# A mixture-of-experts layer: expert rows summed per token in DRAM by scatters that add, and the last stage's odd tiles normed by ScalarE and GpSimd

## The reference

```python
top_logit, top_e = lax.top_k(logits, TOP_K)          # 4 experts per token
gates = jax.nn.softmax(top_logit, axis=-1)
...
xs = xf[tok]                                         # rows sorted by expert
hu = lax.ragged_dot(xs, w_gate_up, group_sizes) + b_gate_up[e_sorted]
gate = jnp.minimum(hu[:, :D_FF], SWIGLU_LIMIT)
up = jnp.clip(hu[:, D_FF:], -SWIGLU_LIMIT, SWIGLU_LIMIT)
act = (up + 1.0) * gate * jax.nn.sigmoid(SWIGLU_ALPHA * gate)
y = lax.ragged_dot(act, w_down, group_sizes) + b_down[e_sorted]
y = y * g_sorted[:, None].astype(y.dtype)
out = jnp.zeros_like(xf).at[tok].add(y)
...
h = layer_norm(ALPHA_RES * h + ffn, ln2_g[l], ln2_b[l])   # ALPHA_RES = 2 ** 0.25
```

## Time and profile before

| what | value |
|---|---|
| time, median of 3 runs | 4528.06 us (4527.1 to 4535.33) |
| profiled execution, span | 4529.3 us |
| PE busy | 4289.9 us (95%) |
| DVE busy | 3076.1 us (68%) |
| ACT busy | 1817.6 us (40%) |
| POOL busy | 1010.1 us (22%) |
| moved by DMA | 665.72 MB, mean 147 GB/s |

### The profile page before, as it was taken

The page is one execution under the profiler, slowest core; times in us unless marked ns, Lnnn a source line. Parts: engine busy times, 40 slices in busy tenths (PEclk is TensorE's granted clock), DMA queues, the critical chain, the costliest instruction groups (busy, mean ns, idle before and its releaser), DMA issues. The chain is left out here.

```text
span 4529.3 us, 70549 instructions
## 1 busy us (share of the span) xinstructions
PE 4289.9 (95%) x24356; PEld 3153.5 (70%) x24356; DVE 3076.1 (68%) x4861; ACT 1817.6 (40%) x2677; POOL 1010.1 (22%) x1152
## 2 busy tenths in 40 slices
PE   8999988999999998699999999999999999999987
PEld 4444434444444454599989889899999999999961
DVE  2587867878888873555556556666676777777768
ACT  1222223443434433233434444444445555555530
POOL 1111101221111122211112212222222222222235
PEclk9999989999999999799999999999999999999986
DMA  6443330120110010544555456474657667667668
GB/s 194 126 122 92 87 101 16 30 27 21 18 23 16 14 27 19 148 158 148 174 168 190 155 183 220 162 250 161 237 197 239 208 230 241 219 234 237 212 214 362
DMA packets 534140, 665.72 MB, mean 147 GB/s; under 512 B 64416, under 2 KB 402592, under 8 KB 533952
## 3 DMA queue, kind: packets, MB, share of 16 engines
q1 hardware_dynamic: 419664, 501.02, 34.7%
q10 hardware_dynamic: 87744, 77.15, 5.4%
q0 software_dynamic: 26576, 85.56, 5.0%
HBM read 543.61 MB, written 120.03 MB: 147 GB/s over the span
## 5 line engine op out<-in xcount | busy, mean ns | idle before, releaser
L2000 PE MATMUL gu<-x_hi,w_hi 128*128 128x240 f32 (+8 forms) x4096 | 1196.5, 292 | 4.1 <-issue 4.1
L2003 PE MATMUL gu<-x_lo,w_hi 128*128 128x240 f32 (+8 forms) x4096 | 1195.5, 292 | 0.5 <-issue 0.5
L2004 PE MATMUL gu<-x_hi,w_lo 128*128 128x240 f32 (+8 forms) x4096 | 1194.1, 292 | 0.0
L2106 DVE TENSOR_TENSOR w_lo<-w_raw,w_hi 128x2048 fp32r<-128x2048 f32 x386 | 874.6, 2287 | 414.1 <-ACT w_hi L2190 386.2
L2190 ACT ACTIVATE w_hi<-w_raw 128x2048 fp32r<-128x2048 f32 x386 | 726.8, 1908 | 207.4 <-PE gu L2004 132.0
L2000 PEld LDWEIGHTS gu<-x_hi,w_hi 128*128 128x128 f32 x4096 | 774.7, 189 | 4.5 <-issue 4.3
L2003 PEld LDWEIGHTS gu<-x_lo,w_hi 128*128 128x128 f32 x4096 | 773.3, 189 | 1.1 <-issue 0.9
L2004 PEld LDWEIGHTS gu<-x_hi,w_lo 128*128 128x128 f32 x4096 | 773.8, 189 | 0.0
L1972 POOL TENSOR_TENSOR a_lo<-up,a_hi 128x384 fp32r<-128x384 f32 x256 | 396.6, 1549 | 1177.8 <-ACT a_hi L2202 1177.8
L570 PE MATMUL proj_acc<-w_in_sb,hT 128*128 128x512 f32 (+1 forms) x1280 | 499.0, 537 | 0.7 <-ACT hT L586 0.7
L2000 PE MATMUL yp<-w_hi,a_hi 128*128 128x512 f32 x1088 | 445.6, 410 | 2.3
(11 more groups left out here) (316 smaller groups left out, 5878.6 us busy)
## 6 DMA issues: line engine op xcount, KB each, us to landing
w_raw<-w_gate_up SPq DMA_DIRECT2D x258, 1024.0 KB, 7.6
w_raw<-w_down SPq DMA_DIRECT2D x128, 1024.0 KB, 8.1
y_dram<-y_rows ACTq DMA_DIRECT2D x128, 256.0 KB, 2.6
y_dram<-zeros ACTq DMA_DIRECT2D x12, 2688.0 KB, 15.5
h_blk<-h_dram SPq DMA_DIRECT2D x32, 512.0 KB, 8.7
qi_dram<-qi_stage ACTq DMA_DIRECT2D x16, 640.0 KB, 3.2
x_in<-x SPq DMA_DIRECT2D x16, 512.0 KB, 6.1
w_in_sb<-w_in SPq DMA_DIRECT2D x4, 2048.0 KB, 14.2
```

The costliest lines, as they stand in the source:

```text
L2000: op = nc.tensor.matmul(out, s_hi_, m_hi, start=(n == 0), stop=False)
L2003: nc.tensor.matmul(out, s_hi_, m_lo, start=False, stop=False)
L2004: op = nc.tensor.matmul(out, s_lo_, m_hi, start=False, stop=(n == len(pairs) - 1))
L2106: nc.vector.tensor_tensor(w_lo[:, c % 2, cols], raw[:, c % 3, cols], w_hi[:, c % 2, cols].bitcast(F32), ALU.subtract).then_inc(s_lo, 1)
```

## The change

- In the attention stage `h1` is stored twice, once into `h1_dram` and once into `sums_dram`, where the experts' rows are to be added. 512 rows of zeros are put behind each of them (for list entries that stand for no token). An entry of `lists` is two numbers, token and gate, 8 bytes; the gates are divided by 2^0.25. The 12 DMAs that wrote zeros over most of `y_dram` in the projection stage are gone, as are `y_dram` and the position lists.
- In a visit, ACT's `store` scales a tile by the gates while copying (`gate_now`). POOL then issues an indirect DMA with `compute_op=ALU.add` that adds each row to its token's row in `sums_dram` (`scatter`; seven a visit, tile 2 by quarter rows). ACT's and SP's stores to `y_dram` are gone.
- The token numbers and gates for the scatters are made by `hold(v)` on POOL, which waits until all scatters of visit v - 1 have landed. `hold(v)` and `gather(v + 1)` stand between `a_lo` of step 2 and of step 3; `gather` stood at the start of the visit.
- SP loads the entries of the last 128 rows (`load_third(v + 1)`, five small DMAs), which waits for `hold(v)`, and stands ahead of chunk 5 of visit v.
- In the last stage a tile is one load from `sums_dram` into one of six buffers; PE adds only the bias rows; DVE does `sums` of all tiles and `finish` of the even ones in two instructions; odd tiles are normed by ACT (one instruction) and POOL (two).

The core of the diff:

```diff
@@ place_stage, weigh and project_stage (cut)
-                    nc.vector.tensor_copy(at_i[:], at_f).then_inc(s_at, 1)
+                    nc.vector.tensor_copy(at_i[:], at_f)
+                    nc.vector.tensor_copy(entry[:, :, 0], token[:, b:b + 1].broadcast_to([P, TOP_E]))
...
+                    nc.vector.tensor_scalar(entry[:, :, 1].bitcast(F32), e_gate, e_inv, 1.0 / ALPHA_RES,
+                                            ALU.mult, ALU.mult).then_inc(s_at, 1)
@@ experts_stage, SP
-                        if not first(v) and c in (3, 4):
-                            store_third(v - 1, 2 if c == 3 else 5)
+                        if c == 5:
+                            load_third(v + 1)
                         chunk(v, c, e)
+                def load_third(v):
+                    at = look_up(sp, v, 1, MOST)
                     rest, few = (look_up(sp, v, what, 1) for what in (2, 3))
+                    if not first(v):
+                        sp.wait_ge(s_hold, v)
                     for i in range(4):
+                        row = at + 2 * P + i * FEW - rest * ((i - i % 2) * FEW) - few * (i % 2 * FEW)
+                        sp.dma_start(third[i * FEW:(i + 1) * FEW], D_["lists"][bass.ds(row, FEW), :]
+                                     ).then_inc(s_third, 16)
+                    sp.dma_start(spot[:], A["spots"][bass.ds(rest + few, 1)].rearrange("o p j n -> (o p) j n")
+                                 ).then_inc(s_third, 16)
@@ experts_stage, POOL
+                def hold(v):
+                    if not first(v):
+                        pool.wait_ge(s_yst[0], 32 * v)
+                        pool.wait_ge(s_yst[1], 32 * v)
+                        pool.wait_ge(s_yst[2], 48 * v)
+                    pool.wait_ge(s_third, 80 * v + 80)
+                    nc.gpsimd.tensor_tensor(scaled[:], spot[:, :, 0], third[:, 0:1].broadcast_to([P, 3]), ALU.mult)
+                    for h in range(2):
+                        nc.gpsimd.tensor_scalar(at_main[:, :, h], who[:, 0:2, 0], 2.0, float(h), ALU.mult, ALU.add)
+                    nc.gpsimd.tensor_copy(gate_now[:, 0:2], who[:, 0:2, 1].bitcast(F32))
+                    nc.gpsimd.tensor_copy(gate_now[:, 2:3], third[:, 1:2].bitcast(F32))
+                    pool.drain()
+                    nc.gpsimd.tensor_tensor(at_third[:], scaled[:], spot[:, :, 1], ALU.add).then_inc(s_hold, 1)
+                    pool.drain()
+                def scatter(v, n):
+                    pool.wait_ge(s_y, 6 * v + n + 3)
+                    nc.gpsimd.tensor_tensor(idle[:, n:n + 1], zero[:, 0:1], zero[:, 0:1], ALU.add)
...
+                        nc.gpsimd.indirect_dma_start(rows, bass.IndirectOffsetOnAxis(ap=at, axis=0), part, None,
+                                                     compute_op=ALU.add).then_inc(s_yst[n % 3], 16)
                 def body(v):
-                    gather(v + 1)
+                    if not first(v):
+                        scatter(v - 1, 5)
                     for j in range(J):
+                        if j == 3:
+                            hold(v)
+                            gather(v + 1)
                         pool.wait_ge(s_ah, 8 * v + j + 1)
...
+                    for n in range(5):
+                        scatter(v, n)
@@ experts_stage, ACT
-                    nc.scalar.activation(y[:, slot], yp[:, n % 2], ACT.Copy).then_inc(s_y, 1)
...
+                    nc.scalar.activation(y[:, slot], yp[:, n % 2], ACT.Copy, scale=gate_now[:, slot:slot + 1]
+                                         ).then_inc(s_y, 1)
@@ combine_stage, SP and POOL
-                            rows[:, t % AHEAD, k], None, D_["y"],
...
+                def root(t):
...
+                    nc.gpsimd.tensor_tensor(shift, mean, rstd, ALU.mult)
+                    pool.drain()
+                    nc.gpsimd.tensor_scalar(shift, shift, -1.0, 1.0, ALU.mult, ALU.mult).then_inc(s_shift, 1)
+                def affine(t):
+                    row = total[:, t % AHEAD]
+                    pool.wait_ge(s_norm, t // 2 + 1)
+                    nc.gpsimd.tensor_tensor(row, row, gain[:], ALU.mult)
+                    pool.drain()
+                    nc.gpsimd.tensor_tensor(row, row, bias[:], ALU.add).then_inc(s_out[1], 1)
                 for t in range(TILES):
+                    root(t)
+                    if t >= 2 and t % 2 == 0:
+                        affine(t - 1)
+                affine(TILES - 1)
@@ combine_stage, DVE
                 def finish(t):
+                    if t % 2:
+                        return
+                    row, slot = total[:, t % AHEAD], t % SUMS
+                    nc.vector.scalar_tensor_tensor(row, row, small[:, slot, 12:13], gain[:], ALU.subtract, ALU.mult)
+                    dve.drain()
+                    dve.wait_ge(s_rstd, t // 2 + 1)
+                    nc.vector.scalar_tensor_tensor(row, row, small[:, slot, 15:16], bias[:], ALU.mult, ALU.add
+                                                   ).then_inc(s_out[0], 1)
```

More of the change, by code:

```diff
@@ L935, in attend_stage @@
         at_f = small[:, 58:62]
[L936 removed]
+        at_i, token, entry = S["at_i"], S["token"], S["entry"]
         e_gate = small[:, 62:66]
@@ L1979, in _ @@
                 n = over_visits(pool, body)
+                scatter(n - 1, 5)
                 pool.wait_ge(s_x, 48 * n + 48)
-                nc.gpsimd.tensor_tensor(who_now[:], who[:], zero[:], ALU.add)
+                pool.wait_ge(s_yst[0], 32 * n)
+                pool.wait_ge(s_yst[1], 32 * n)
+                pool.wait_ge(s_yst[2], 48 * n)
+                pool.wait_ge(s_third, 80 * n + 80)
+                nc.gpsimd.tensor_tensor(who_now[:], who[:, :, 0], zero[:], ALU.add)
             @block.tensor
@@ new lines, in root @@
+                def root(t):
+                    slot = t % SUMS
+                    mean, var_eps, rstd, shift = (small[:, slot, n:n + 1] for n in (12, 14, 15, 16))
+                    pool.wait_ge(s_var, t + 1)
+                    op = nc.gpsimd.tensor_tensor(rstd, var_eps, minus_half[:], ALU.pow)
+                    if t % 2 == 0:
+                        op.then_inc(s_rstd, 1)
+                        return
+                    pool.drain()
+                    nc.gpsimd.tensor_tensor(shift, mean, rstd, ALU.mult)
+                    pool.drain()
+                    nc.gpsimd.tensor_scalar(shift, shift, -1.0, 1.0, ALU.mult, ALU.mult).then_inc(s_shift, 1)
@@ L2428, in _ @@
                                          ).then_inc(s_bts, 1)
+                for t in range(1, TILES, 2):
+                    row, slot = total[:, t % AHEAD], t % SUMS
+                    act.wait_ge(s_shift, t // 2 + 1)
+                    nc.scalar.activation(row, row, ACT.Identity, bias=small[:, slot, 16:17],
+                                         scale=small[:, slot, 15:16]).then_inc(s_norm, 1)
 def build(nc, A, upto=9):
```

287 lines of the change are left out of this document (100 added, 187 removed).

## The result

The changed kernel takes 4540.4 us (median of six runs, 4531.6 to 4545.7), the kernel before 4528.8 us in the same comparison; the ratio is 1.0023, with a 95% interval of 1.0013 to 1.0033. The forecast was 4515 us and faster. The time lies inside the range, and the sign is wrong.

A forecast was written before the change was run, and what follows sets the result against it. PE alone was taken to hold the experts stage, the DMA engines the last stage. Terms +1 +4 +13 +0 +2 -33 = -13 us on the span of 4529.3 gave 4516.3, stated as 4515; range 4486 to 4562.

The forecast's parts named there:

- One visit, POOL: Experts stage, moved fetch on POOL: +1.1 us in each of 12 narrow visits, sum +13 us, bounds 0 and +85.
- the term `hold`: POOL, ahead of the fetch in a visit: six small instructions and two drains, about 1.2 us.
- the 12.0 us: POOL between steps 2 and 3: `hold`, look-up, row fetches, `a_lo` and `a_rest` together, releasing step 3's `a_lo` at 4141.1.
- d: Lateness of DVE's `up` of step 5 in a narrow visit: 1.7 us, said as 1.9 with one wait of `who_now`.
- 0.80 us of slack: DVE's idle time ahead of `gate` of step 7 in a narrow visit, taken off the lateness: chain end 1.1 us late.
- Visits of other widths: Wider visits of the experts stage: longer steps give 1.6 us of slack, so no cost; nothing changes in visits of 77.8 us.
- The rows' arrival: Narrow visit: third fetch lands at 4147.5 against the transposes at 4149.40; nothing, at most 0.6 us inside the 1.1.
- the scatters: Experts stage: landing taken as 6 us, no cost per visit; the last one waited for at the end, +2, bounds 0 and +6.
- Start: Start of the experts stage: five DMAs 3.0 us and look-ups 1.5, less two selects 0.7; +4, bounds 0 to +8.
- The last stage: Expert-row fetches go and a pair of tiles takes 11.0 us: -33 us, bounds -50 and -28.
- the mutual block: Last stage: POOL's affine and DVE's finish block each other, a pair taking 11.0 us instead of 8.6.
- the fetch rival: Step 3's `a_lo` late as `hold` meets `w_lo`: 3.1 us a narrow visit, 41 instead of 13, 4543; chance 0.27.

The follow-up runs named there:

- the writing scatter: Changed kernel with the scatters writing instead of adding (`compute_op=ALU.add` left out): 4536.3 us, ratio 1.0004 to the kernel before.
- the kernel before with `hold`'s like: Kernel before with the next visit's fetch moved to step 3, behind small operations and drains as in `hold` on unread tiles: 4578.0 us, ratio 1.0102.

## Why the prediction was wrong

**The step that failed is "One visit, POOL", and in it the term `hold`.** It was costed as six small instructions and two drains, 1.2 us; in every narrow visit it took 3.45. Of the 2.25 us between, 0.7 are there without any meeting (1.92 us in the wider visits, 0.98 of it idle ahead of the instruction behind the drain), and 1.5 come from meeting DVE, above all the `w_lo`. The other terms of the 12.0 us were right within 0.5: look-up 1.60 against 1.5, `who` to the first row 3.67 against 4.15, three fetches 3.74 against 3.9. So d was 3.35 and not 1.9, and each narrow visit lost 3.0 us and not 1.1. The mechanism was the one forecast (step 3's `a_rest` late, DVE's `up` of step 5 behind it, 0.80 us of slack, PE's wait put down to `a_rest`). That this place alone makes the loss is shown from both sides: put into the kernel before it costs 5 us a narrow visit, and spread in the changed kernel 0.1 to 0.35 are left.

The prediction had the case among its rivals, with 3.1 us for a narrow visit and 1.4 for the next width, 41 us in all; measured were 3.0, 0.4 and 38.8 (35.8 up to the last visit, and its own 3.0). It weighed it low by one sentence: "by my count `hold` is through 0.1 us before" the `w_lo` that blocks. By its own numbers that is not so: `a_rest` of step 2 ended at 4129.09, 1.2 us more is 4130.3, and the `w_lo` began at 4130.11. And it put next to nothing for the drain, behind which the last instruction stands 0.98 us idle. A margin of 0.1 us in a sum of operations that the trace doesn't have is no margin: with the 1.92 us of the wider visits `hold` would end at 4131.0, in the middle of that `w_lo`, and the rival was the forecast. As for the rule of the Trainium skill's page "SBUF — State Buffer", section "Who interferes with whom", that the later of the two engines waits for the whole instruction of the other: the trace agrees: `at_third`, 0.20 us without a `w_lo` beside it, took 1.22 and ended with `w_lo` (4154.32 and 4154.26).

**Visits of other widths**: those of 77.83 us unchanged, as forecast; the width of 256 lost 0.4.

**The rows' arrival, the scatters**: neither is what PE waits for; the scatter lands in 7.4 to 7.6 us (median; the longest found in any of these traces is 10.2) against the 6 estimated, under the 12.4 from which it would cost. The end of the stage took +4 for it and not +2; the writing scatter shows that 3 of it are the addition. The Trainium skill's page "Collectives: The Full Stack", section "Stop ④ — SDMA + CCE: where bytes move and the add happens", has one pass with two reads; in these runs that pass lands in 7.6 us against 5.7 without the addition.

**Start**: +4 was forecast, +1.2 is in the profile once attention's own spread is taken out. The five small DMAs took 2.72 us (SP, 1851.96 to 1854.68), as forecast (3.0); where the 1.5 us of look-ups went the rows don't show:

```profile
1851.96 2.17 SPq L1901 DMA_DIRECT2D third<-lists_dram  x4
1854.33 0.35 SPq L1903 DMA_DIRECT2D spot<-spots  x1
1854.88 1.03 SPq L1884 DMA_DIRECT2D w_raw<-w_gate_up  x2
```

**The last stage** is the part that was right in size: -37 against -33. Pairs came every 10.6 to 10.9 us (11.0 forecast), the first in 8.7, by the mutual block; the chain that ended last (start us, us) runs over POOL with its two affine rows and the drain behind the root (L2328), which the count had not had:

```profile
4448.90 2.32 POOL total L2336
4451.35 3.36 POOL total L2338
4454.71 1.49 POOLq L2328
4456.89 1.97 issue
4459.45 2.31 POOL total L2336
```

The affine row of 3.36 us in place of 2.35 and DVE's finish of 2.24 us on average in place of 1.28 are the two sides of the block. The first sum came 11.5 us after the start of the stage; since the forecast took it from before's bias matmuls, which end 13.35 us after it, this is 1.9 of the 4 us that the stage gave beyond the forecast. It was luck: those of before ran at a granted clock of 0.50, and these at 1.00.

**The range** held the time, since its upper reach was set by the fetch rival. That reach was itself mis-added: with the +85 us that the prediction gives as the bound of this term, instead of its +13, the sum is 4587 and not 4562.

**Span and median.** The forecast of 4515 missed the median of 4540.4 by 25 us. In the profile 14 of them are seen (a span of 4530.1 against 4516.3), +26 from the visits and +2 from the end of the stage, less 4 from the last stage, 3 from the start and 7 from attention. The other 11 to 12 are that the prediction put the median 1.2 us under the span, while this profile was the shortest of its runs, at the highest clock.

## What to carry to other kernels

Work that moves to an engine "with time to spare" has to be summed per step, at the step whose result somebody waits for, with drains and with each possible meeting with a VectorE instruction of two SBUF inputs counted whole; busy shares say nothing on it. When such a step is full, moving one part to another single step may not be enough (`hold` at step 1 gave back 10 of 37 us); spreading the work over four steps turned a loss of 0.2% into a gain of 0.7%. Compare stages between profiles with the granted clock beside them. And when a stage gets short by losing its traffic, check by undoing the other edits of the same stage whether they gave anything.

## What the runs showed of the hardware

- The same wide visits ran faster in the kernel before with `hold`'s like than in any other program: 76.25 us instead of 77.83, and 97.3 instead of 98.7 us, at the same granted clock of 1.00 in that stretch. The matmuls of 272 columns follow each other there every 123.6 ns instead of 126.9, those of 256 every 113.6 instead of 120.2, and those of 240 every 112.6 instead of 113.5, apart from one wait of 0.9 us a visit; those of 336 columns are slower (156.0 instead of 153.3). The kernel before with the fetch alone moved has a little of it (visits of 77.3 us). PE's instructions were not edited. What sets this isn't settled; it is some 19 us in all, so a comparison of totals between programs can hide a gain or a loss of half a per cent, and stage by stage it shows.
- An indirect DMA that adds holds POOL 1.58 us for each issue against 0.99 without the addition.
- A one-element operation on POOL (`idle`) took 0.19 us alone and up to 2.1 us when it met DVE; a row fetch 1.0 and up to 2.87.
- Runs of one kernel differ with the mean granted clock of TensorE: 4529.7 to 4531.7 us at 0.973 and 0.974, 4551.1 at 0.968, for the changed kernel.
